# A 128x128 triangular inverse computed as two 64x64 diagonal blocks and one block below them

## The chip, the cores and the metric

One core of a Trainium2 chip runs the whole kernel. The metric is device time in microseconds (us), the median of three runs. Five engines work beside each other, each on its own queue of instructions and held by semaphores only: TensorE (PE, its weight loads shown apart as PEld), VectorE (DVE), ScalarE (ACT), GpSimd (POOL) and SyncE (SP), which issues the DMAs.

## What is computed

The reference is three layers over 256 tokens of width 1024: latent attention with a feed-forward part, differential attention with a feed-forward part, and a hybrid layer. The change is in the hybrid layer's delta rule, which works on 8 heads in chunks of 128 tokens, two chunks to a head:

```
m = jnp.where(strict, jnp.einsum('bhnid,bhnjd->bhnij', k_beta, kc) * decay, 0.0)
a_mat = m + jnp.eye(c, dtype=m.dtype)
rhs = jnp.concatenate([vc * bc[..., None], k_beta * jnp.exp(G)[..., None]], axis=-1)
sol = lax.linalg.triangular_solve(a_mat, rhs, left_side=True, lower=True, unit_diagonal=True)
u, w = sol[..., :dv], sol[..., dv:]
```

`a_mat` is 128x128, lower triangular with ones on the diagonal. All is float32.

## The kernel before

Everything is written out by hand per engine: each engine has a list of steps, the order in the code is its queue, and the steps wait on counters. Big projections split both operands into a high and a low float32r part (ScalarE writes `high`, line 342, VectorE or GpSimd writes `low`, line 349) and run three matmuls for each 128 rows of contraction (line 1508 in the delta-rule stage).

The delta rule goes over four pairs of heads, so four matrices at a time (two heads, two chunks). The inverse is made in the kernel by doubling: with the inverse of the diagonal blocks of size s known, the block below each is filled in. `inv` holds four inverses and, in its other half, their transposes. `masked_dve` makes the masked matrices `mk`, TensorE turns them (`turn_m_pe`), ScalarE copies them to `mt`. The blocks of size 2 need no matmul: a mask (`level1`) and a subtraction from the identity, for the inverses by GpSimd (`init_pool`, lines 1732 and 1735), for the transposes by VectorE (`init_dve`, lines 1697 and 1698). Then come six levels. A level is: x group (`level_x`, line 1745, four products of `mt` and `inv`), a masked copy by VectorE (`level_xm`, line 1758), t group (`level_t`, lines 1752 and 1753, eight products, four in the last level), and a subtraction by VectorE (`level_tt`, line 1763). Each product is 128x128x128 in plain float32.

While VectorE works between two groups, TensorE does half a projection of the next pair (`gdn_block`, 12 instructions), or of the following attention stage in the last pair. So `pair_pe` weaves groups and half projections, and `pair_dve` weaves the level steps with the convolution of the next pair. Behind the levels stand the state's matmuls (`f1` to `f4`), the output's norm and gate (`ogn`, line 1976; `og`, line 1984), and then, for the next pair, mask, turn and start values. TensorE fills the wait for these with matmuls that nobody reads (`spin`, line 482). Pairs run through `over`, a loop of the queue: the first pair and the last one or two are written out, the rest is the loop's body.

On GpSimd the end of a pair is: a power (line 2034), the low part of a weight chunk (slot 3), `init_pool`, `grow_pool` (`qdec_t`, line 1724), the low part of the next chunk (slot 4), the output's low part (`obl`, line 2047).

Of the kernel before, what the change touches and what calls it, by code (L numbers as in the profile page):

```python
# [23 lines left out]
P = 128  # L24
TOK = 256
# [17 lines left out]
LEVELS = 6  # L43

# [67 lines left out]
for _n, _w in (("ident", P), ("upper", P), ("strict_lower", P), ("level1", P), ("level1_t", P),  # L112
               ("levels", LEVELS * P), ("ones", P), ("causal", 3 * P), ("dist", NT * TOK),
               ("mla_cos", NT * MLA_ROPE), ("mla_sin", NT * MLA_ROPE), ("mla_rot", TOK),
               ("att_cos", NT * 2 * ROT), ("att_sin", NT * 2 * ROT)):
    _const(_n, _w)
# [3 lines left out]
def constants():  # L120
# [12 lines left out]
    def level(s):  # L133
        return (r // (2 * s) == k // (2 * s)) & (r % (2 * s) >= s) & (k % (2 * s) < s)

    put("level1", level(1))
    put("level1_t", level(1).T)
    put("levels", np.stack([level(2 << n) for n in range(LEVELS)], 1))
# [112 lines left out]
def build(nc, dram, y_out):  # L251
# [66 lines left out]
    def repeat(ap, n):  # L318

        return ap.unsqueeze(1).to_broadcast([P, n, ap.shape[1]])  # L320
# [1167 lines left out]
    level_of = cst("levels", "p (l k) -> p l k", l=LEVELS)  # L1488
# [76 lines left out]
    def is0(j):  # L1565
        return isinstance(j, int) and j == 0
# [126 lines left out]

    def init_dve(dve, j):
# [31 lines left out]
    def init_pool(pool, j):  # L1726

        pool.wait_ge(e_["mk"], j + 1)
        if not is0(j):
            pool.wait_ge(e_["f3"], j)  # L1730
        for e in range(2):
            last = pool.tensor_tensor(bm[:, 0, 2 * e:2 * e + 2, :], mk[:, e, 0, :, :], repeat(cst("level1"), NT), ALU.mult)
        last.then_inc(e_["bm"], 1)
        pool.wait_ge(e_["bm"], j + 1)
        pool.tensor_tensor(inv[:, 0, :, :], repeat(ident, 4), bm[:, 0, :, :], ALU.subtract).then_inc(e_["init_g"], 1)
# [12 lines left out]
    def level_t(pe, l, j):  # L1748
        pe.wait_ge(e_["xm"], LEVELS * j + l + 1)
        for c in range(4):  # L1750
            if l < LEVELS - 1:
                pe.matmul(A[2][:, c * P:(c + 1) * P], inv[:, 1, c, :], xm[:, c, :], start=True, stop=True)  # L1752
            last = pe.matmul(A[3][:, c * P:(c + 1) * P], xm[:, c, :], inv[:, 1, c, :], start=True, stop=True)  # L1753
        last.then_inc(e_["t"], 1)

    def level_xm(dve, l, j):
        dve.wait_ge(e_["x"], LEVELS * j + l + 1)
        dve.tensor_tensor(xm[:], quad(A[0]), repeat(level_of[:, l, :], 4), ALU.mult).then_inc(e_["xm"], 1)

    def level_tt(dve, l, j):  # L1760
        dve.wait_ge(e_["t"], LEVELS * j + l + 1)
        if l < LEVELS - 1:
            dve.tensor_tensor(inv[:].rearrange("p a c k -> p (a c k)"), inv[:].rearrange("p a c k -> p (a c k)"),
                              acc[:, 2:4, :].rearrange("p a b -> p (a b)"), ALU.subtract).then_inc(e_["tt"], 1)
        else:
            dve.tensor_tensor(inv[:, 1, :, :], inv[:, 1, :, :], quad(A[3]), ALU.subtract).then_inc(e_["tt"], 1)

    def pair_pe(pe, i):
# [13 lines left out]
        for e in range(2):  # L1782
            pe.matmul(A[0][:, e * P:(e + 1) * P], inv[:, 1, 2 * e, :], vbeta[:, 2 * e, :], start=True, stop=True)
        for e in range(2):
            last = pe.matmul(A[0][:, (2 + e) * P:(3 + e) * P], kbg[:, e, :], inv[:, 1, 2 * e + 1, :], start=True, stop=True)
# [14 lines left out]
        for e in range(2):  # L1800
            pe.matmul(A[0][:, e * P:(e + 1) * P], inv[:, 1, 2 * e + 1, :], vbeta[:, 2 * e + 1, :], start=True, stop=False)
            last = pe.matmul(A[0][:, e * P:(e + 1) * P], nwt[:, e, :], state[:, e, :], start=False, stop=True)
# [34 lines left out]
    def gdn_pe(pe):  # L1837
# [17 lines left out]
        over(pe, PAIRS, lambda i: pair_pe(pe, i))  # L1855
# [78 lines left out]
    def pair_dve(dve, i):  # L1934
# [42 lines left out]
        if more:  # L1977
            masked_dve(dve, i + 1)
        dve.wait_ge(e_["ot"], i + 1)
# [12 lines left out]
    def gdn_dve(dve):  # L1992
# [22 lines left out]
        masked_dve(dve, 0)  # L2015
        init_dve(dve, 0)
        over(dve, PAIRS, lambda i: pair_dve(dve, i), 2)

    def pair_pool(pool, i):
# [15 lines left out]
        if more:  # L2035
            refill(split, *source(3, 0, i + 1))
            init_pool(pool, i + 1)
# [11 lines left out]
    def gdn_pool(pool):  # L2049
# [9 lines left out]
        init_pool(pool, 0)  # L2059
# [624 lines left out]
```

## Time and profile before

| | us |
|---|---|
| median of three runs (1153.77 to 1156.37) | 1155.96 |
| the profiled execution | 1154.09 |
| its span | 1152.0 |
| TensorE busy | 1080.5 |
| VectorE busy | 696.5 |
| GpSimd busy | 428.6 |
| levels and starts of the four pairs | 729.7 to 929 of the span |

The profiled execution is one run; its span is from the first to the last recorded instruction. A row of a timeline gives the start in the span, the length, engine, line, operation, out<-in, the shape, and in brackets how long the engine stood idle before it and who released it. TensorE's instructions are pipelined, so that they overlap in their stamped lengths.

### The profile page before, as it was taken

What the parts mean: (1) busy time and instruction counts of PE and PEld (TensorE: products, weight loads), DVE (VectorE), ACT (ScalarE), POOL (GpSimd) and SP (SyncE); (2) the same over time, 40 slices, a digit from 0 to 9 for tenths busy, and PEclk for the clock granted to TensorE, in tenths of its full rate; (3) what the DMA queues carried; (4) which work ended last, traced back from release to release, by engine and by line L of the source; (5) the groups of instructions that cost most, each with busy time, mean ns of one, the idle gap of its engine ahead of it and who ended that gap; (6) DMA issues with size and microseconds to landing.
All of it is one profiled execution on the core that took longest, in us unless ns stands there. A gap on an engine that the chain in (4) does not pass through costs nothing.

```text
span 1152.0 us, 20992 instructions
## 1 busy us (share of the span) xinstructions
PE 1080.5 (94%) x7752; PEld 996.5 (86%) x7752; DVE 696.5 (60%) x1058; ACT 563.4 (49%) x1028; POOL 428.6 (37%) x296
## 2 busy tenths in 40 slices
PE   5699999999999998999999997989899999999997
PEld 5599699999978997699999966888888999999996
DVE  4455767667666556666766567566666555554444
ACT  4345565555555655555555555333333235544442
POOL 1000224333342332243343545647363345544331
PEclk9899999999999999999999999999999999999999
DMA  8233366565534442556555333131312234445551
GB/s 336 72 114 112 140 204 193 182 205 185 180 110 144 140 136 74 183 185 198 187 189 172 128 110 128 38 111 37 110 41 69 80 106 164 146 146 188 187 188 40
DMA packets 46256, 162.94 MB, mean 141 GB/s; under 512 B 5248, under 2 KB 5504, under 8 KB 46080
## 3 DMA queue, kind: packets, MB, share of 16 engines
q1 hardware_dynamic: 44768, 157.05, 40.8%
q0 software_dynamic: 1440, 5.24, 1.4%
q8 instruction: 31, 0.51, 0.2%
q14 instruction: 17, 0.14, 0.0%
HBM read 161.22 MB, written 1.05 MB: 141 GB/s over the span
## 4 chain that ended last, share of the span: by engine, by line
PE 83%; DVE 9%; ACT 3%; POOL 2%; issue 2%; DMA 1%; DVEq 0%; POOLq 0%; ACTq 0%
PE work L377 13%; PE work L379 13%; PE work L378 13%; PE acc L377 5%; PE acc L378 5%; PE acc L379 5%; PE work L1508 5%; PE work L2095 4%; PE work L2107 2%; PE acc L1745 2%; PE acc L1753 2%; DVE silu L1553 2%; PE acc L2107 1%; DVE conv L1543 1%; PE acc L1752 1%
## 5 line engine op out<-in xcount | busy, mean ns | idle before, releaser
L349 POOL TENSOR_TENSOR low<-raw,high 128x1024 fp32r<-128x1024 f32 x109 | 265.7, 2439 | 336.2 <-ACT high L342 336.2
L349 DVE TENSOR_TENSOR low<-raw,high 128x1024 fp32r<-128x1024 f32 (+2 forms) x191 | 277.8, 1463 | 166.3 <-ACT high L342 166.2
L342 ACT ACTIVATE high<-raw 128x1024 fp32r<-128x1024 f32 (+4 forms) x301 | 306.1, 1025 | 45.9 <-DMA raw<-in_w_out 21.9
L377 PE MATMUL work<-xh,high 128*128 128x256 f32 (+1 forms) x1032 | 292.2, 283 | 0.3 <-DVE low L349 0.3
L378 PE MATMUL work<-xl,high 128*128 128x256 f32 (+1 forms) x1032 | 288.7, 280 | 0.0
L379 PE MATMUL work<-xh,low 128*128 128x256 f32 (+1 forms) x1032 | 288.5, 280 | 0.0
L377 PEld LDWEIGHTS work<-xh,high 128*128 128x128 f32 (+1 forms) x1032 | 194.0, 188 | 5.3 <-issue 2.9
L378 PEld LDWEIGHTS work<-xl,high 128*128 128x128 f32 (+1 forms) x1032 | 194.1, 188 | 2.5 <-issue 0.7
L379 PEld LDWEIGHTS work<-xh,low 128*128 128x128 f32 (+1 forms) x1032 | 194.0, 188 | 0.2
L1044 POOL TENSOR_TENSOR h<-gelu,cv 128x256 f32<-128x256 f32 x44 | 48.8, 1108 | 200.5 <-ACT gelu L964 106.7
L1508 PE MATMUL work<-xh,high 128*128 128x256 f32 x256 | 76.9, 301 | 3.6 <-DVE hn L1563 2.0
L1508 PE MATMUL work<-xl,high 128*128 128x256 f32 x256 | 72.0, 281 | 0.0
L1508 PE MATMUL work<-xh,low 128*128 128x256 f32 x256 | 71.8, 281 | 0.0
L377 PE MATMUL acc<-high,hh 128*128 128x512 f32 x168 | 65.9, 392 | 1.2 <-DVE low L349 1.2
L378 PE MATMUL acc<-low,hh 128*128 128x512 f32 x168 | 65.8, 392 | 0.0
L379 PE MATMUL acc<-high,hl 128*128 128x512 f32 x168 | 65.4, 389 | 0.0
L970 ACT ACTIVATE hh<-h 128x256 fp32r<-128x256 f32 x44 | 18.4, 418 | 70.1 <-POOL h L1044 70.1
L1508 PEld LDWEIGHTS work<-xh,high 128*128 128x128 f32 x256 | 49.0, 192 | 4.2 <-issue 2.2
L958 ACT ACTIVATE cv<-work,vec 128x256 f32<-128x256 f32 x44 | 24.8, 564 | 51.0 <-PE work L379 51.0
L1508 PEld LDWEIGHTS work<-xl,high 128*128 128x128 f32 x256 | 48.9, 191 | 0.0
L1508 PEld LDWEIGHTS work<-xh,low 128*128 128x128 f32 x256 | 48.7, 190 | 0.0
L1046 POOL TENSOR_TENSOR hl<-h,hh 128x256 fp32r<-128x256 f32 x44 | 34.0, 773 | 24.4 <-ACT hh L970 24.4
(364 smaller groups left out, 2345.7 us busy)
## 6 DMA issues: line engine op xcount, KB each, us to landing
raw<-in_w_ffn SPq DMA_DIRECT2D x132, 512.0 KB, 4.2
raw<-in_w_out SPq DMA_DIRECT2D x39, 512.0 KB, 4.1
raw<-in_w_diff SPq DMA_DIRECT2D x32, 512.0 KB, 3.9
raw<-in_w_att SPq DMA_DIRECT2D x32, 512.0 KB, 3.8
raw<-in_w_gdn SPq DMA_DIRECT2D x24, 512.0 KB, 3.4
raw<-in_w_mla SPq DMA_DIRECT2D x8, 512.0 KB, 3.3
raw<-in_w_gdnz SPq DMA_DIRECT2D x8, 512.0 KB, 4.5
raw<-in_w_mla SPq DMA_DIRECT2D x8, 384.0 KB, 3.1
```

The lines of the kernel that those rows point to most:

```text
L342: act.activation(high[k][:, 0:w], raw[k][:, 0:w], ACT.Copy).then_inc(high_done[k], 1)
L349: eng.tensor_tensor(low[k][:, 0:w], raw[k][:, 0:w], high[k][:, 0:w], ALU.subtract).then_inc(low_done[k], 1)
L377: pe.matmul(out, lhs[0], rhs[0], start=start, stop=False)
L378: pe.matmul(out, lhs[0], rhs[1], start=False, stop=False)
L379: return pe.matmul(out, lhs[1], rhs[0], start=False, stop=stop)
L958: act.activation((cg, cv)[value][j][:], W[bank][:, 0:TOK], ACT.Identity, scale=ffn_taps(layer, i, j, value, 1, 0), bias=ffn_taps(layer, i, ...
L1044: pool.tensor_tensor(h32[j][:], gelu[j][:], cv[j][:], ALU.mult).then_inc(s["h32"], 1)
L1046: pool.tensor_tensor(hl[j][:], h32[j][:], hh[j][:], ALU.subtract).then_inc(s["hl"], 1)
L1508: last = pe.matmul(W[x][:, 0:TOK], l[slot][:, b * P:(b + 1) * P], r[:, b, :], start=(s == 0), stop=(s == 23))
L1553: dve.scalar_tensor_tensor(silu2[:, 3 * e + x, :], tanh_[x][:], 1.0, conv[x][:], ALU.add, ALU.mult).then_inc(taps[x]["silu"], 1)
L2095: last = pe.matmul(W[0][:, t * TOK:(t + 1) * TOK], x[:, b, t * P:(t + 1) * P], w[k][:, o:o + TOK], start=(b == 0 and term == 0), stop=(b = ...
L2107: last = pe.matmul(out, w[k][:, b * P:(b + 1) * P], x[:, b, :], start=(s == 0), stop=(s == 23))
```

## The change

The 128x128 inverse is now two inverses of 64x64, on partitions 0 to 63 and 64 to 127, and one block below. The levels up to 64 treat the two diagonal blocks as separate 64x64x64 products: the lower half of the partitions uses rows and columns 0 to 63 of TensorE's array, the upper half 64 to 127. `inv`, `xm` and the masks have 64 columns in place of 128, so VectorE's masked copy and subtraction cover half the elements; both results of a t group lie in one PSUM bank. The last level fills the one lower block: four products in its x group, four in its t group, an unmasked copy, and a multiply by -1 into `inv_t`, a new 128x128 tile of the transposed inverses. Its diagonal blocks are copied from `inv` at the end of the fifth level, and its zero block is set once.

The rows' start values move from GpSimd (`init_pool`, gone) to VectorE (`init_rows_dve`, directly behind `masked_dve`). Steps that mask a diagonal block are now two instructions of 64 partitions. TensorE's pairs are written out four times in place of the loop.

```diff
-                  "levels", LEVELS * P                     (each level's mask 128 wide)
+                  "levels", (LEVELS - 1) * HALF            (64 wide; ident_half, level1, level1_t too)
-    inv = sb("inv", [P, 2, 4, P])
+    inv = sb("inv", [P, 2, 4, HALF])
+    inv_t = sb("inv_t", [P, 4, P])
-    xm = sb("xm", [P, 4, P])
+    xm = sb("xm", [P, 4, HALF])
+    def init_rows_dve(dve, j):
+        dve.wait_ge(e_["mk"], j + 1)
+        for h_ in HALVES:
+            last = dve.tensor_tensor(bm[h_, 0, :, 0:HALF]..., mk[h_, :, 0, :, h_], cst("level1")[h_, :]..., ALU.mult)
+        last.then_inc(e_["bm"], 1)
+        dve.wait_ge(e_["bm"], j + 1)
+        dve.tensor_tensor(inv[:, 0, :, :], repeat(cst("ident_half"), 4), bm[:, 0, :, 0:HALF],
+                          ALU.subtract).then_inc(e_["init_g"], 1)
     def init_dve(dve, j):
         dve.wait_ge(e_["mtev"], j + 1)
-        chain(dve.tensor_tensor(bm[:, 1, :, :], mt[:], repeat(cst("level1_t"), 4), ALU.mult))
-        chain(dve.tensor_tensor(inv[:, 1, :, :], repeat(ident, 4), bm[:, 1, :, :], ALU.subtract))
+        if is0(j):
+            dve.memset(inv_t[HALF:P, :, 0:HALF], 0.0)
+        for h_ in HALVES:
+            last = dve.tensor_tensor(bm[h_, 1, :, 0:HALF], mt[h_, :, h_], repeat(cst("level1_t")[h_, :], 4), ALU.mult)
+        chain(last)
+        chain(dve.tensor_tensor(inv[:, 1, :, :], repeat(cst("ident_half"), 4), bm[:, 1, :, 0:HALF], ALU.subtract))
-    def init_pool(pool, j):
...
     def level_x(pe, l, j):
+        lower, upper = HALVES
         for c in range(4):
-            last = pe.matmul(A[0][:, c * P:(c + 1) * P], mt[:, c, :], inv[:, 0, c, :], start=True, stop=True)
+            at = slice(c * HALF, (c + 1) * HALF)
+            if l < LEVELS - 1:
+                for h_ in HALVES:
+                    last = pe.matmul(A[0][h_, at], mt[h_, c, h_], inv[h_, 0, c, :], start=True, stop=True)
+            else:
+                last = pe.matmul(A[0][upper, at], mt[lower, c, upper], inv[lower, 0, c, :], start=True, stop=True)
     def level_t(pe, l, j):
         for c in range(4):
+            at, at_t = slice(c * HALF, (c + 1) * HALF), slice((4 + c) * HALF, (5 + c) * HALF)
             if l < LEVELS - 1:
-                pe.matmul(A[2][:, c * P:(c + 1) * P], inv[:, 1, c, :], xm[:, c, :], start=True, stop=True)
-            last = pe.matmul(A[3][:, c * P:(c + 1) * P], xm[:, c, :], inv[:, 1, c, :], start=True, stop=True)
+                for h_ in HALVES:
+                    pe.matmul(A[2][h_, at], inv[h_, 1, c, :], xm[h_, c, :], start=True, stop=True)
+                for h_ in HALVES:
+                    last = pe.matmul(A[2][h_, at_t], xm[h_, c, :], inv[h_, 1, c, :], start=True, stop=True)
+            else:
+                last = pe.matmul(A[2][lower, at], xm[upper, c, :], inv[upper, 1, c, :], start=True, stop=True)
     def level_tt(dve, l, j):
+            if l == LEVELS - 2:
+                dve.wait_ge(e_["tt"], LEVELS * j + l + 1)
+                for h_ in HALVES:
+                    dve.tensor_copy(inv_t[h_, :, h_], inv[h_, 1, :, :])
         else:
-            dve.tensor_tensor(inv[:, 1, :, :], inv[:, 1, :, :], quad(A[3]), ALU.subtract).then_inc(e_["tt"], 1)
+            dve.tensor_scalar(inv_t[0:HALF, :, HALF:P], quad_half(A[2][0:HALF, 0:4 * HALF]), -1.0, None,
+                              ALU.mult).then_inc(e_["tt"], 1)
-        over(pe, PAIRS, lambda i: pair_pe(pe, i))
+        for i in range(PAIRS):
+            pair_pe(pe, i)
         if more:
             masked_dve(dve, i + 1)
+            init_rows_dve(dve, i + 1)
         if more:
             refill(split, *source(3, 0, i + 1))
-            init_pool(pool, i + 1)
             grow_pool(pool, i + 1)
```

TensorE, the t group of a level and the last instruction of the half projection ahead of it. Before:

```order
L1508 MATMUL work<-xh,low 128x256
L1752 MATMUL acc<-xm,inv 128x128
L1753 MATMUL acc<-inv,xm 128x128
L1752 MATMUL acc<-xm,inv 128x128
L1753 MATMUL acc<-inv,xm 128x128
```

And now:

```order
L1516 MATMUL work<-xh,low 128x256
L1771 MATMUL acc<-xm,inv 64x64 x2
L1773 MATMUL acc<-inv,xm 64x64 x2
L1771 MATMUL acc<-xm,inv 64x64 x2
L1773 MATMUL acc<-inv,xm 64x64 x2
```

Each 128x128 product has become two of 64x64, first the one on the lower half, then the one on the upper; the half projections around them stay where they were. (A row is a product; each is two instructions on the engine.)

VectorE, from the output's norm to the start values of the next pair. Before:

```order
L1976 TENSOR_TENSOR ogn<-acc,root 128x512
L1690 TENSOR_TENSOR mk<-acc,mask_e 128x512 x2
L1984 SCALAR_TENSOR_TENSOR og<-acc,gdn_gain,hn 128x512
L1563 SCALAR_TENSOR_TENSOR hn<-tanh,work 128x256
L1697 TENSOR_TENSOR bm<-mt,const 128x512
L1698 TENSOR_TENSOR inv<-const,bm 128x512
```

And now:

```order
L1698 TENSOR_TENSOR mk<-acc,mask_e 128x512 x2
L1705 TENSOR_TENSOR bm<-mk,const 64x4x64 x2
L1709 TENSOR_TENSOR inv<-const,bm 128x256
L2017 SCALAR_TENSOR_TENSOR og<-acc,gdn_gain,hn 128x512
L1571 SCALAR_TENSOR_TENSOR hn<-tanh,work 128x256
L1718 TENSOR_TENSOR bm<-mt,const 64x4x64 x2
L1720 TENSOR_TENSOR inv<-const,bm 128x256
```

Three instructions have come in ahead of the gated output `og`, and the columns' start values are three instructions in place of two.

GpSimd at the same place. Before:

```order
L2034 TENSOR_TENSOR root<-mean,vec 128x4
L349 TENSOR_TENSOR low<-raw,high 128x1024
L1732 TENSOR_TENSOR bm<-mk,const 128x256 x2
L1735 TENSOR_TENSOR inv<-const,bm 128x512
L1724 TENSOR_TENSOR qdec_t<-silu,grown_all 128x256
L349 TENSOR_TENSOR low<-raw,high 128x1024
L2047 TENSOR_TENSOR obl<-og,obh 128x512
```

And now:

```order
L2068 TENSOR_TENSOR root<-mean,vec 128x4
L352 TENSOR_TENSOR low<-raw,high 128x1024
L1746 TENSOR_TENSOR qdec_t<-silu,grown_all 128x256
L352 TENSOR_TENSOR low<-raw,high 128x1024
L2080 TENSOR_TENSOR obl<-og,obh 128x512
```

The two steps of the start values are gone, so the second low part and the steps behind it have moved up.

## Rows read from the trace of the kernel before

**Rows 1.** The page: engine totals, and the last chain's shares by engine.

```profile
PE 1080.5 (94%) x7752; PEld 996.5 (86%) x7752; DVE 696.5 (60%) x1058; ACT 563.4 (49%) x1028; POOL 428.6 (37%) x296
...
PE 83%; DVE 9%; ACT 3%; POOL 2%; issue 2%; DMA 1%; DVEq 0%; POOLq 0%; ACTq 0%
```

**Rows 2.** Grouped lines, TensorE, the inversion: xcount | busy us, mean ns | idle before.

```profile
L1753 PE MATMUL acc<-inv,xm 128*128 128x128 f32 x192 | 35.1, 275 | 0.0
L1752 PE MATMUL acc<-xm,inv 128*128 128x128 f32 x160 | 30.9, 275 | 0.0
...
L1745 PE MATMUL acc<-inv,mt 128*128 128x128 f32 x192 | 27.5, 286 | 2.1 <-DVE inv L1763 1.3 <-DVE inv L1698 0.8
```

**Rows 3.** Timeline, TensorE, one level of pair 0: start us, length us, instruction.

```profile
735.29 1.16 PE L1745 MATMUL acc<-inv,mt 128*128 128x128 f32 x8
...
737.71 0.38 PE L1752 MATMUL acc<-xm,inv 128*128 128x128 f32 x2
...
739.27 0.39 PE L1753 MATMUL acc<-inv,xm 128*128 128x128 f32 x2
...
740.97 1.16 PE L1745 MATMUL acc<-inv,mt 128*128 128x128 f32 x8
```

**Rows 4.** Timeline, TensorE: two 16-row transposes between projection instructions.

```profile
683.41 0.28 PE L1508 MATMUL work<-xl,high 128*128 128x256 f32 x1
683.53 0.27 PE L1508 MATMUL work<-xh,low 128*128 128x256 f32 x1
683.74 0.29 PE L1381 MATMUL work<-const,junk 16*128 16x16 f32 x2
683.96 0.39 PE L1508 MATMUL work<-xh,high 128*128 128x256 f32 x1
684.18 0.28 PE L1508 MATMUL work<-xl,high 128*128 128x256 f32 x1
```

**Rows 5.** Waits of TensorE, 726 to 937 us: us in total, times, longest.

```profile
PE acc L1745 <- DVE inv L1763: 1.3, 3, 0.4
PE acc L1745 <- DVE inv L1698: 0.8, 2, 0.5
```

**Rows 6.** Timeline, VectorE, between pairs 0 and 1.

```profile
778.35 1.28 DVE L1690 TENSOR_TENSOR mk<-acc,mask_e 128x512 f32<-128x512 f32 x2
780.15 0.75 DVE L1984 SCALAR_TENSOR_TENSOR og<-acc,gdn_gain,hn 128x512 f32<-128x512 f32 x1 [0.53 <-PE acc L1827]
780.82 0.41 DVE L1563 SCALAR_TENSOR_TENSOR hn<-tanh,work 128x256 f32<-128x256 f32 x1
781.56 1.77 DVE L1697 TENSOR_TENSOR bm<-mt,const 128x512 f32<-128x512 f32 x1 [0.33 <-ACT mt L1635]
783.37 1.09 DVE L1698 TENSOR_TENSOR inv<-const,bm 128x512 f32<-128x512 f32 x1
```

**Rows 7.** Timeline, TensorE, the filler between these pairs and the x group behind it.

```profile
780.39 3.60 PE L482 MATMUL acc<-const 128*128 128x512 f32 x8
784.52 0.38 PE L1745 MATMUL acc<-inv,mt 128*128 128x128 f32 x1 [0.53 <-DVE inv L1698]
```

**Rows 8.** Timeline, TensorE's weight loads, two products with 16 moving columns.

```profile
695.66 0.31 PEld L1386 LDWEIGHTS work<-gate_g,const 128*128 128x128 f32 x2
695.88 0.30 PEld L1387 LDWEIGHTS work<-gate_g,const 128*128 128x128 f32 x2
```

**Rows 9.** Timeline, ScalarE, two places: before the transposes, between the pairs.

```profile
681.04 0.37 ACT L1397 ACTIVATE junk<-work 16x256 f32<-16x256 f32 x1 [3.99 <-PE work L379]
...
779.99 1.05 ACT L342 ACTIVATE high<-raw 128x1024 fp32r<-128x1024 f32 x1
```

**Rows 10.** Timeline, GpSimd, between pairs 0 and 1.

```profile
777.67 2.38 POOL L349 TENSOR_TENSOR low<-raw,high 128x1024 fp32r<-128x1024 f32 x1
780.02 1.41 POOL L1732 TENSOR_TENSOR bm<-mk,const 128x256 f32<-128x256 f32 x2
781.51 1.27 POOL L1735 TENSOR_TENSOR inv<-const,bm 128x512 f32<-128x512 f32 x1
782.75 1.17 POOL L1724 TENSOR_TENSOR qdec_t<-silu,grown_all 128x256 f32<-128x256 f32 x1
783.88 2.81 POOL L349 TENSOR_TENSOR low<-raw,high 128x1024 fp32r<-128x1024 f32 x1
```

**Rows 11.** Busy us of a stretch: length, engines, granted clock, DMA share, GB/s.

```profile
828.00:831.40 3.40, 3.40 (x20) 3.40 (x18) 1.01 (x3) 1.23 (x3) 0.00 (x0) 0.55 0.16 61
```

More of the change, by code:

```diff
@@ L43 @@
 LEVELS = 6
+HALF = 64
 class Phase:
@@ L109, in _const @@
     CONST[name] = (sum(w for _, w in CONST.values()), width)
-for _n, _w in (("ident", P), ("upper", P), ("strict_lower", P), ("level1", P), ("level1_t", P),
-               ("levels", LEVELS * P), ("ones", P), ("causal", 3 * P), ("dist", NT * TOK),
+for _n, _w in (("ident", P), ("upper", P), ("strict_lower", P), ("ident_half", HALF), ("level1", HALF),
+               ("level1_t", HALF), ("levels", (LEVELS - 1) * HALF), ("ones", P), ("causal", 3 * P), ("dist", NT * TOK),
                ("mla_cos", NT * MLA_ROPE), ("mla_sin", NT * MLA_ROPE), ("mla_rot", TOK),
@@ L133, in level @@
     def level(s):
-        return (r // (2 * s) == k // (2 * s)) & (r % (2 * s) >= s) & (k % (2 * s) < s)
+        full = (r // (2 * s) == k // (2 * s)) & (r % (2 * s) >= s) & (k % (2 * s) < s)
+        return full[:, 0:HALF] | full[:, HALF:P]
+    put("ident_half", (r == k)[:, 0:HALF] | (r == k)[:, HALF:P])
     put("level1", level(1))
-    put("level1_t", level(1).T)
-    put("levels", np.stack([level(2 << n) for n in range(LEVELS)], 1))
+    put("level1_t", np.concatenate([level(1)[0:HALF].T] * 2))
+    put("levels", np.stack([level(2 << n) for n in range(LEVELS - 1)], 1))
     put("ones", np.ones((P, P)))
@@ L318, in repeat @@
     def repeat(ap, n):
-        return ap.unsqueeze(1).to_broadcast([P, n, ap.shape[1]])
+        return ap.unsqueeze(1).to_broadcast([ap.shape[0], n, ap.shape[1]])
     landed = [sem(f"landed{k}") for k in range(6)]
@@ L1487, in build, with quad_half @@
     A = [acc[:, k, :] for k in range(4)]
-    level_of = cst("levels", "p (l k) -> p l k", l=LEVELS)
+    level_of = cst("levels", "p (l k) -> p l k", l=LEVELS - 1)
+    HALVES = (slice(0, HALF), slice(HALF, P))
+    def quad_half(a):
+        return a.rearrange("p (c k) -> p c k", c=4)
     BLOCKS = [(0, 0), (1, 0), (2, 0), (0, 1), (1, 1), (2, 1)]
@@ L1724, in grow_pool @@
         pool.tensor_tensor(qdec_t[:], qk_t[:, :, 1, :], g2, ALU.mult).then_inc(e_["grown"], 1)
-    def init_pool(pool, j):
[L1728 to L1735, printed above, removed]
     def level_x(pe, l, j):
@@ L1749, in level_t @@
         pe.wait_ge(e_["xm"], LEVELS * j + l + 1)
+        lower, upper = HALVES
         for c in range(4):
+            at, at_t = slice(c * HALF, (c + 1) * HALF), slice((4 + c) * HALF, (5 + c) * HALF)
             if l < LEVELS - 1:
[L1752 to L1753 removed]
+                for h_ in HALVES:
[4 more added lines that the diff above has]
+                last = pe.matmul(A[2][lower, at], xm[upper, c, :], inv[upper, 1, c, :], start=True, stop=True)
         last.then_inc(e_["t"], 1)
@@ L1757, in level_xm @@
         dve.wait_ge(e_["x"], LEVELS * j + l + 1)
-        dve.tensor_tensor(xm[:], quad(A[0]), repeat(level_of[:, l, :], 4), ALU.mult).then_inc(e_["xm"], 1)
+        if l < LEVELS - 1:
+            dve.tensor_tensor(xm[:], quad_half(A[0][:, 0:4 * HALF]), repeat(level_of[:, l, :], 4),
+                              ALU.mult).then_inc(e_["xm"], 1)
+        else:
+            dve.tensor_copy(xm[HALF:P, :, :], quad_half(A[0][HALF:P, 0:4 * HALF])).then_inc(e_["xm"], 1)
     def level_tt(dve, l, j):
@@ L1782, in pair_pe @@
         for e in range(2):
-            pe.matmul(A[0][:, e * P:(e + 1) * P], inv[:, 1, 2 * e, :], vbeta[:, 2 * e, :], start=True, stop=True)
+            pe.matmul(A[0][:, e * P:(e + 1) * P], inv_t[:, 2 * e, :], vbeta[:, 2 * e, :], start=True, stop=True)
         for e in range(2):
-            last = pe.matmul(A[0][:, (2 + e) * P:(3 + e) * P], kbg[:, e, :], inv[:, 1, 2 * e + 1, :], start=True, stop=True)
+            last = pe.matmul(A[0][:, (2 + e) * P:(3 + e) * P], kbg[:, e, :], inv_t[:, 2 * e + 1, :], start=True, stop=True)
         last.then_inc(e_["f1"], 1)
@@ L1800, in pair_pe @@
         for e in range(2):
-            pe.matmul(A[0][:, e * P:(e + 1) * P], inv[:, 1, 2 * e + 1, :], vbeta[:, 2 * e + 1, :], start=True, stop=False)
+            pe.matmul(A[0][:, e * P:(e + 1) * P], inv_t[:, 2 * e + 1, :], vbeta[:, 2 * e + 1, :], start=True, stop=False)
             last = pe.matmul(A[0][:, e * P:(e + 1) * P], nwt[:, e, :], state[:, e, :], start=False, stop=True)
@@ L2015, in gdn_dve @@
         masked_dve(dve, 0)
+        init_rows_dve(dve, 0)
         init_dve(dve, 0)
```

5 lines of the change are left out of this document (3 added, 2 removed).

## The prediction, made before the changed kernel ran

> **What bounds the kernel now.** I read the page from the top: TensorE is busy 94% of the span and carries 83% of the chain that ended last, VectorE 9% [rows 1]. So most of what leaves TensorE shortens the run, and what VectorE loses counts only where TensorE waits for it. The grouped lines give the part that the change touches: the three matmul lines of the inversion are 192 + 160 + 192 = 544 TensorE instructions, two for each float32 product [rows 2]. Then the timeline of one level, from one x group to the next (735.29 to 740.97, 5.68 us) [rows 3]: x group, half a projection (12 instructions), t group, half a projection. From 737.71 to 739.27 lie 14 instructions of the t group: 1.56 / 14 = 0.1114 us each. The stamped length of an instruction is more than twice that, since they are pipelined; pace is what counts. A projection instruction has a pace of 0.117 us (683.41 to 683.53 and its neighbours) [rows 4]. A level thus holds 24 x 0.1114 + 24 x 0.117 = 5.48 us of work and 0.20 us of gaps. The reader is to see that VectorE is almost never the limit inside a level: in the whole stage TensorE waited 1.3 us in three places for the subtraction that ends a level [rows 5]. Between two pairs it is different: VectorE's chain runs there (mask, gated output, start values), and the first x group starts 0.53 us late behind it [rows 6, 7].
>
> **The change, part by part.** Durations are of the profiled execution, 1154.09 us (span 1152.0); the three timed runs have a median of 1155.96, 1.87 above it.
>
> *Matmuls of the levels.* 544 instructions of 128 by 128 become (5 x 24 + 8) x 2 x 4 = 1024 of 64 by 64: four pairs, 24 products in each of five levels, 8 in the last. What has to be known is the pace of a small one, and no row shows it. The nearest rows: a product with only 16 moving columns, but 128 columns of weights, still goes at 0.11 us (two weight loads from 695.66, the next two from 695.88) [rows 8]. So a full float32 instruction is held by its weight load as much as by its 128 moving columns, and both halve at 64. Lower bound: the loads and matmuls of opposite corners run side by side, a quarter of the pace, 0.028. Upper bound: an instruction costs 0.111 whatever its size. I take half the pace, 0.0555, loads passing one behind another, because [rows 8] are the only ones where something small was tried and there the load set the pace. 1024 x 0.0555 = 56.8 against 544 x 0.1114 = 60.6: -3.8 us (bounds -31.9 and +53.1).
>
> *Changing the shape of the array.* Each x and t group is now an island of corner products between full-size projections, 2 x 6 x 4 = 48 islands. One island stands in the trace: two transposes of 16 rows between projection instructions [rows 4]. Their ScalarE input was ready 2.3 us before (681.04 + 0.37) [rows 9], so it is not a wait. From the last projection before (683.53) to the second behind (684.18) pass 0.65 us; 0.117 + 2 x 0.11 + 0.117 = 0.46 would do. So 0.19 us for in and out: 48 x 0.19 = 9.1 us. The 0.20 of gaps in 20 levels (4.0) and the waits of 1.3 go into that, the waits because the subtraction has half the elements (1024 to 512). Net +3.8 us. Matmuls and islands together: 0.0 us.
> The Trainium skill, "TensorEngine Tiling (Array Packing)", section Tiling Modes, Key Properties, speaks against the change: a switch of the tiling mode drains TensorE. The 0.19 is less than two whole drains: an instruction is stamped 0.28 and paced 0.12, so a full one would be 0.16 at each end and 96 of them 15.4 us in place of 9.1. By the page the time would be some 6 us above mine; the row decides.
>
> *Start values move from GpSimd to VectorE.* Before, GpSimd masks the rows' start values (two parts of bm, then inv) while VectorE goes on to the gated output and the columns' start values [rows 6, 10]. Now VectorE does both, in the order mask, rows' values (three instructions), gated output, gate product, columns' values (three). Each of the six has half the elements of one of 128x512, whose pace is 0.6 (two in 1.28) [rows 6]: half of that and a little for the start, 0.34 each, an estimate. All six read two SBUF operands, and the rows show what that means beside GpSimd: VectorE's bm at 781.56 took 1.77 us, until GpSimd's inv (781.51 + 1.27) was done, GpSimd's next then took 1.17 for 256 elements, and its 1024-column subtraction at 783.88 took 2.81, the end of VectorE's inv (784.46) plus 2.25 [rows 6, 10]. They take turns, instruction by instruction. Worked through for pair 0 to 1: the mask ends at 779.63; GpSimd's subtraction holds on to 780.05; first row part to 780.39, GpSimd's qdec_t to 780.98, second row part to 781.32; then GpSimd's next subtraction, no longer behind its own start values and ready with ScalarE's high part (779.99 + 1.05 = 781.04) [rows 9], holds to 783.57; rows' inv to 783.9; gated output 784.6; gate product 785.0; columns' values 786.1, or 787.3 if GpSimd's last step of the pair (obl) falls between. The x group started at 784.52, so it starts 1.6 to 2.8 us later; I take +2.0 for this and the next pair, and +1.0 for the third, where no second subtraction of that slot stands on GpSimd (the weights of slot 4 end there). +5.0 us. If nothing collides, the x group stands right behind the filler (780.39 + 8 x 0.43 = 783.83; the 0.43 from 3.60 less the last one's tail, over 8) [rows 7]: bound -0.8, the waits for inv that the stage has now [rows 5]. Upper bound: 2 x 2.8 + 1.3 = 6.9, and if TensorE's clock falls behind the longer wait, as its grant stood at a mean of 0.55, nearly all at 1.2 GHz, for 3.4 us between pairs 1 and 2 [rows 11], 1.7 us each: 12. Queued behind the six on VectorE is the whole pair: TensorE's x group, then everything. Before pair 0 the same work is hidden by the filler, with no GpSimd work left beside it.
>
> *At nothing.* VectorE's xm and subtraction at half size: covered already by a 1.4 us half projection; without that cover they would be worth 0.9 a level. The two copies to inv_t in level 4 lie under the following half projection. GpSimd's three instructions less: it only makes its next subtraction earlier, counted above. TensorE's pairs written out four times: the loop's branch lay behind the filler; cost 0, bounds 1 us either way. The constants' DMA is smaller, at the start, beside other loads.
>
> Sum: -3.8 + 3.8 + 5.0 = +5.0 us: 1159.1 on the profiled run, 1161.0 on the median.
>
> **The rivals.**
> *A, the corners work side by side (faster).* The products alternate between the two corners, which share neither rows nor columns nor output partitions. If both weight loads and matmuls of the two overlap, the pace falls to 0.028 and the levels to 1024 x 0.028 = 28.7: -31.9 + 3.8 + 5.0 = -23, 1133. With some issue cost left, 0.034: 34.8, -17, 1139; 0.04: 1145. It decides from a pace below 0.0506 on, where the levels have paid for the starts of the pairs. For it: rows of the array are only read by their own corner, and a level of 4.5 us would still leave VectorE and ScalarE time. Against: [rows 8], one load behind the other; and the two instructions of a product lie next to each other on the same corner.
> The Trainium skill, "TensorEngine Tiling (Array Packing)", Key Properties, has this rule: different tiles can load weights and multiply in parallel. No run here shows it; by it the time would be this rival's.
> *B, a small instruction has a price of its own.* If the pace does not fall below 0.07 to 0.08: +11 to +21 for the matmuls, 1175 to 1186 in all, taken as 1181. For it: load and matmul of 64 columns are two issues each in 0.0555 us, and no two in the trace are that close. Against: nothing in the rows looks like an issue limit.
> *C, VectorE is not held.* GpSimd's subtraction comes later or elsewhere; the starts of the pairs gain 0.8, the levels are even: 1155.2, no change.
>
> **How the numbers follow.** Forecast 0.42, its own range 1152 to 1173 (paces 0.052 to 0.060: -3.6 to +4.6; pair starts from -0.8 to 12). A 0.36, B 0.14, C 0.08. Predicted 1161.0. Range 1132 to 1174: it leaves out the best end of A (0.04), nearly all of B (0.12) and 0.02 of the forecast. Some 0.2% (2.3 us) is what a measurement can tell from no change. Faster: 0.35 of A, 0.03 of C, 0.01 of the forecast: 0.39. Same: 0.01 of A, 0.05 of C, 0.05 of the forecast: 0.11. Slower: 0.36 and B: 0.50.
>
> **What would show it.** The t group of a level (32 instructions): 1.78 us if the pace is 0.0555, about 0.9 in A, over 2.2 in B. The distance from x group to x group: 5.68 now, about 5.7 here, 4.5 in A. The island's edges: weight loads of the first projection instruction behind a t group start after it, not during it. Between pairs: VectorE's rows' values with spans well over 0.4 us, the first x group 4 us or more behind the filler's last instruction. Wrong I am if the t group's starts come in twos, or if VectorE's six instructions show their bare 0.4.

## The result

| kernel | us, median | range | runs | ratio to before, 95% interval |
|---|---|---|---|---|
| before | 1155.31 | 1153.77 to 1156.37 | 4 | |
| changed | 1147.03 | 1145.71 to 1148.30 | 4 | 0.9929 [0.9912, 0.9947] |

The change is faster by 8.3 us, where 1161.0 was forecast: the range held the time, the direction was wrong. A second, longer comparison gave the same (1147.11, 0.9931 [0.9912, 0.9950], label e10_after_again below).

The profiled execution of the changed kernel took 1148.30 us, its span 1146.5. Its page answers to [rows 1]; TensorE has more instructions (8232) and less busy time:

```profile
PE 1069.9 (93%) x8232; PEld 978.2 (85%) x8232; DVE 694.3 (61%) x1083; ACT 563.5 (49%) x1028; POOL 415.5 (36%) x284
```

A row of a timeline stands for instructions that the profile has put together: in x4 below, four, two products. TensorE in pair 0, which answers to [rows 3]: from the last projection instruction ahead of the first level's t group to the x group of the third level.

```profile
734.46 0.28 PE L1516 MATMUL work<-xh,low 128*128 128x256 f32 x1
734.67 0.33 PE L1771 MATMUL acc<-xm,inv 64*64 64x64 f32 x4
734.84 0.28 PE L1773 MATMUL acc<-inv,xm 64*64 64x64 f32 x4
...
735.54 0.28 PE L1773 MATMUL acc<-inv,xm 64*64 64x64 f32 x4
735.75 0.39 PE L1516 MATMUL work<-xh,high 128*128 128x256 f32 x1
735.97 0.28 PE L1516 MATMUL work<-xl,high 128*128 128x256 f32 x1
...
737.37 0.68 PE L1759 MATMUL acc<-inv,mt 64*64 64x64 f32 x16
737.98 0.39 PE L1516 MATMUL work<-xh,high 128*128 128x256 f32 x1
...
742.29 0.68 PE L1759 MATMUL acc<-inv,mt 64*64 64x64 f32 x16
```

Four instructions start every 0.117 us (734.84 to 735.54 is 24 instructions in 0.70): **0.029 us each**, about a quarter of the 0.1114 before, not half. The single records behind these rows start in twos, one on each corner: 734.779 and 734.786, then 734.838 and 734.844. A level is 742.29 - 737.37 = 4.92 us long, 5.68 before. The islands cost more than forecast: from 734.46 to 735.97 pass 1.51 us, of which two projection steps (0.234) and 32 x 0.029 = 0.93 are work, so that 0.35 is the way in and out.

The last level has its products on one corner only. In the x group of that level 8 instructions take as long as 16 on two corners (757.05 to 757.65, against 737.37 to 737.98):

```profile
756.84 0.28 PE L1516 MATMUL work<-xh,low 128*128 128x256 f32 x1
757.05 0.67 PE L1761 MATMUL acc<-inv,mt 64*64 64x64 f32 x8
757.65 0.39 PE L1516 MATMUL work<-xh,high 128*128 128x256 f32 x1
```

Between the pairs it went the other way. TensorE's waits in the stage (728 to 937 us; us in total, times, longest), against the 0.8 and 1.3 of [rows 5]:

```profile
PE acc L1759 <- DVE inv L1720: 7.1, 3, 3.1
PE work L1591 <- DVE silu L1561: 5.7, 3, 1.9
```

The second was there before too. The first is new: VectorE's start values are late, by 3.07, 3.07 and 0.99 us. VectorE between pairs 0 and 1, which answers to [rows 6]:

```profile
777.93 1.55 DVE L1705 TENSOR_TENSOR bm<-mk,const 64x256 f32<-64x256 f32 x2
779.52 2.50 DVE L1709 TENSOR_TENSOR inv<-const,bm 128x256 f32<-128x256 f32 x1
...
783.80 1.37 DVE L1720 TENSOR_TENSOR inv<-const,bm 128x256 f32<-128x256 f32 x1
```

and GpSimd beside it, which answers to [rows 10]:

```profile
779.38 2.35 POOL L352 TENSOR_TENSOR low<-raw,high 128x1024 fp32r<-128x1024 f32 x1 [0.18 <-ACT high L345]
783.42 1.47 POOL L2080 TENSOR_TENSOR obl<-og,obh 128x512 fp32r<-128x512 f32 x1 [1.69 <-ACT obh L1935]
```

L1709 and L1720, of 128x256, take 2.50 and 1.37 us, and each ends 0.3 us after the GpSimd instruction beside it (781.73, 784.89).

The stage by its pairs, from the first x group of one pair to that of the next, and in the last pair to the x group of the last level: 54.78, 56.16, 55.44 and 29.44 before, 52.87, 54.29, 53.18 and 25.92 now, 9.6 us less in all. The medians differ by 8.3. The rest lies outside the stage. What comes ahead of it differs between the profiles by up to 5 us in both directions: the stage of this profile began 2.7 us later than that of before, that of another changed version (e8 below) 0.2 earlier. What comes behind it took 1.3 us more than before in this profile.

### The profile page after: what moved, and what is told of

Its sections match the earlier page's. It is cut to its first block, busy times and chain, and to the rows that moved or that the text cites. A ratio compares the mean times of both kernels' runs of the same rounds, so it can differ in the third digit from the quotient of the medians.

```text
span 1146.5 us, 21927 instructions
## 1 busy us (share of the span) xinstructions
PE 1069.9 (93%) x8232; PEld 978.2 (85%) x8232; DVE 694.3 (61%) x1083; ACT 563.5 (49%) x1028; POOL 415.5 (36%) x284
## 4 chain that ended last, share of the span: by engine, by line
PE 81%; DVE 8%; issue 4%; POOL 3%; ACT 3%; DMA 1%; DVEq 0%; POOLq 0%; ACTq 0%
PE work L380 13%; PE work L381 13%; PE work L382 13%; PE work L1516 6%; PE acc L380 5%; PE acc L381 5%; PE acc L382 5%; PE work L2127 4%; PE work L2139 3%; PE acc L2139 1%; POOL low L352 1%; PE acc L1771 1%; PE acc L1759 1%; PE work L1137 1%; PE acc L1773 1%
```

## The experiments

Nine runs follow; e10 is the changed kernel once more. "Before" in each row of this table is the median of the kernel before on the same chip.

| label | us, median | range | before | ratio, 95% interval |
|---|---|---|---|---|
| e1_corners_apart | 1169.1 | 1166.99 to 1170.1 | 1155.07 | 1.0117 [1.0095, 1.0139] |
| e2_before_rows_vector | 1165.95 | 1165.34 to 1168.63 | 1155.07 | 1.0101 [1.0078, 1.0124] |
| e3_rows_gpsimd | 1140.51 | 1140.06 to 1141.23 | 1155.07 | 0.9875 [0.9855, 0.9894] |
| e4_gpsimd_later | 1144.19 | 1143.6 to 1145.16 | 1155.07 | 0.9908 [0.9891, 0.9925] |
| e5_corner_island | 1162.44 | 1162.28 to 1164.93 | 1154.81 | 1.0064 [1.0047, 1.0081] |
| e6_full_island | 1157.05 | 1153.03 to 1157.84 | 1154.81 | 1.0014 [1.0003, 1.0026] |
| e8_silu_free | 1129.5 | 1129.15 to 1131.73 | 1154.81 | 0.9785 [0.9767, 0.9804] |
| e9_before_silu_free | 1146.32 | 1143.57 to 1147.47 | 1155.54 | 0.9915 [0.9885, 0.9944] |
| e10_after_again | 1147.11 | 1145.91 to 1151.19 | 1155.54 | 0.9931 [0.9912, 0.9950] |

The theory after the result: the two corners load and multiply side by side, which is worth more than the islands and the late starts cost together; all three are real and separate.

### Do the corners work side by side, or is a small product just quick? (e1)

The changed kernel, with all products of the lower corner first and then all of the upper one, in the five levels that have both. The work is the same, only neighbours in the queue are on one corner.

```diff
+        for h_ in HALVES if l < LEVELS - 1 else ():
             for c in range(4):
                 at = slice(c * HALF, (c + 1) * HALF)
-                for h_ in HALVES:
-                    last = pe.matmul(A[0][h_, at], mt[h_, c, h_], inv[h_, 0, c, :], ...)
+                last = pe.matmul(A[0][h_, at], mt[h_, c, h_], inv[h_, 0, c, :], ...)
     (level_t likewise)
```

> The changed kernel, but in the first five levels all products of the lower corner are issued first, then all of the upper one. Theory (the two corners work side by side when neighbours in the queue lie on opposite corners; one corner alone has a pace of 0.058 us an instruction, as the last level's x group suggests, 8 instructions on one corner in the time of 16 on two): the pace goes from 0.029 to 0.058, 48 x 0.029 = 1.4 us a level, 20 levels: +28 us on 1147, about 1175; a t group's instructions take 1.8 us in place of 0.93. Rival (a 64x64 instruction costs 0.029 by its size alone, wherever it lies): no change, 1147.

It took 1169.1 us, 22 more than the changed kernel: 20 levels at 1.00 us more each, and in its stage five stretches of some 3.4 us at a granted clock of 0.50 (1.2 GHz) in place of three. A level of pair 0:

```profile
736.83 0.96 PE L1758 MATMUL acc<-inv,mt 64*64 64x64 f32 x16
737.72 0.38 PE L1516 MATMUL work<-xh,high 128*128 128x256 f32 x1
...
739.49 0.28 PE L1771 MATMUL acc<-inv,xm 64*64 64x64 f32 x2
739.61 0.28 PE L1770 MATMUL acc<-xm,inv 64*64 64x64 f32 x2
...
742.75 0.96 PE L1758 MATMUL acc<-inv,mt 64*64 64x64 f32 x16
```

Now two instructions start in each 0.117 us, 0.058 each, and the level is 742.75 - 736.83 = 5.92 us long, longer than before the change. So the gain below half of a full instruction comes not from the small product but from its neighbour on the other corner. (Whether two corners that share rows or columns would do the same, no run shows.) The run came out 6 us below the theory's 1175, and the trace shows where: in the middle of the t group, where the queue passes from the lower corner to the upper one, eight instructions take 0.29 us in place of 0.47:

```profile
740.07 0.33 PE L1770 MATMUL acc<-xm,inv 64*64 64x64 f32 x4
740.19 0.33 PE L1771 MATMUL acc<-inv,xm 64*64 64x64 f32 x4
740.36 0.28 PE L1770 MATMUL acc<-xm,inv 64*64 64x64 f32 x2
```

The two corners overlap there for once. 0.18 us in each of 40 groups are 7.2 us.

### What does the move of the rows' start values cost by itself? (e2)

The kernel before, with `init_pool` called on VectorE behind `masked_dve`, at its full width, ahead of pair 0 too; nothing else is changed.

```diff
     (pair_dve)     masked_dve(dve, i + 1)
+                   init_pool(dve, i + 1)
     (pair_pool)    refill(split, *source(3, 0, i + 1))
-                   init_pool(pool, i + 1)
```

> The kernel before, with one part of the change alone: the rows' start values move from GpSimd to VectorE, at full width (three more VectorE instructions between mask and gated output). Theory (VectorE is held there by GpSimd's second subtraction, which has moved up): the first x group of pairs 1 to 3 starts 3 to 4 us behind the filler twice and about 2 once, 8 us in all, and a half-clock stretch may follow: 1163 to 1167 on 1155.3. Rival (only VectorE's own added work counts, 2 x 0.34 + 0.6 = 1.3 a pair): +4, 1159.

1165.95 us, 10.9 over before. TensorE's wait for the start values in the stage, and the longest row of VectorE between pairs 0 and 1:

```profile
PE acc L1745 <- DVE inv L1698: 8.0, 3, 3.3
```
```profile
780.98 2.76 DVE L1735 TENSOR_TENSOR inv<-const,bm 128x512 f32<-128x512 f32 x1
```

Waits of 8.0 against 0.8 are 7.2 us; behind two of the late starts the granted clock then lies at 0.50, 1.2 GHz, for 3.4 us (from 787.1 and from 848.6), and its stage holds four such stretches where before has two. This part of the change loses time on its own.

### The same taken back in the changed kernel (e3), and GpSimd's subtraction alone moved (e4)

e3 gives the rows' start values back to GpSimd, at the new half size and at their old place in its list; its `init_rows_pool` also waits for GpSimd's own step ahead of each of its steps. e4 leaves them on VectorE and only puts GpSimd's second subtraction (slot 4) behind `obl`.

```diff
 e3, pair_dve:
-            init_rows_dve(dve, i + 1)
 e3, pair_pool:
+            init_rows_pool(pool, i + 1)
             grow_pool(pool, i + 1)
 e4, pair_pool:
             grow_pool(pool, i + 1)
-            refill(split, *source(3, 1, i + 1))
         ...
         pool.tensor_tensor(obl[:, pair, :], og32[:], obh[:, pair, :], ALU.subtract).then_inc(e_["ol"], 1)
+        if more:
+            refill(split, *source(3, 1, i + 1))
```

> The changed kernel, but the rows' start values are on GpSimd again, ahead of qdec_t as before, at half size. Theory (held by GpSimd's subtraction): the waits of 7.1 us before the first x groups fall to about 1, and the half-clock stretches behind them go, 1.5 each: about 1139 against 1147. Rival (VectorE's own work, 3 x 0.34 = 1.0 a pair): -3, 1144.

> The changed kernel with VectorE's work untouched; on GpSimd the second subtraction of a pair's end (the low part of slot 4) stands behind the output's low part, so it can't fall between VectorE's start values. Theory (it is that subtraction that holds VectorE): the waits of 3.07 us at the starts of pairs 1 and 2 fall to about 0.5, the third (0.99, no such subtraction) stays, half-clock stretches go: 1140 to 1142. Rival (VectorE's own work): 1147.

e3 took 1140.51, 6.5 less than the changed kernel, and the 7.1 us of waits for the start values are gone: the x group (784.74) stands right behind the filler (781.21, 3.60 long). The low clock, which was expected to go too, did not: e3 has three such stretches in the stage as the changed kernel has, all behind the waits for `silu`. e4 took 1144.19, 2.8 less. VectorE in e4, and TensorE's wait:

```profile
781.62 0.43 DVE L1709 TENSOR_TENSOR inv<-const,bm 128x256 f32<-128x256 f32 x1
...
783.83 1.37 DVE L1720 TENSOR_TENSOR inv<-const,bm 128x256 f32<-128x256 f32 x1
```
```profile
PE acc L1759 <- DVE inv L1720: 2.9, 3, 1.0
```

L1709 has fallen from 2.50 to 0.43 without a change of its own: GpSimd's subtraction held it. No semaphore stands between the two, so "held by semaphores only", said of the engines at the start, is not the whole of it. The rest of the wait, 0.9 to 1.0 at each of the three starts, is VectorE's own three instructions, of which the two of L1705 still take 1.50 us beside `qdec_t`, and `obl`, which still lies beside L1720; how it divides among them, no run shows. e4 missed its 1140 to 1142 by 2 us. Waits of 2.9 us were left where 2.0 had been counted, and the low clock did not go: e4 too has three stretches in the stage, all behind the waits for `silu`.

### What does an island cost? (e5, e6)

The changed kernel, with one more product that nobody reads in the middle of each of the 36 half projections of pairs 0 to 2: in e5 of 64x64 on the lower corner, in e6 with weights of 128x128 and 64 moving columns.

```diff
     (gdn_block, behind the sixth group of three)
+  e5:  pe.matmul(A[3][0:HALF, 0:HALF], cst("ident")[0:HALF, 0:HALF], cst("ident")[0:HALF, 0:HALF], ...)
+  e6:  pe.matmul(A[3][:, 0:HALF], ident, cst("ident")[:, 0:HALF], ...)
```

> The changed kernel with one more 64x64 product, read by nobody, in the middle of each of the 36 half projections that are woven into the levels of pairs 0 to 2: 36 new islands, with no wait in them. Theory (the 0.345 us that an island costs in the trace of the changed kernel is the change of the array's shape itself): 36 x (0.345 + 2 x 0.058) = 16.6 us, 1163.6. Rival (the edge costs the 0.19 us of the prediction, and the rest of the 0.345 was a wait for VectorE's masked copy or subtraction): 36 x (0.19 + 0.116) = 11 us, 1158. In the timeline: two projection instructions around the product 0.58 us apart against 0.42.

> The same place and count, but the product has weights of the full 128x128 and 64 moving columns, so that the array keeps its shape. Theory (only the change of shape costs): 36 x 2 x 0.117 = 8.4 us at most, 1155.4, less if 64 columns are quicker than 128. Rival (any foreign float32 product between the projections costs an edge, whatever its shape): the same as with the small product, 1158 to 1164.

e5 and e6 took 15.4 and 10.0 us more than the changed kernel, 0.43 and 0.28 for each product. The timeline tells them apart more sharply. e5, the step before the product to the second behind:

```profile
738.77 0.28 PE L1518 MATMUL work<-xh,low 128*128 128x256 f32 x1
738.98 0.32 PE L1517 MATMUL acc<-const 64*64 64x64 f32 x2
739.24 0.38 PE L1518 MATMUL work<-xh,high 128*128 128x256 f32 x1
739.46 0.28 PE L1518 MATMUL work<-xl,high 128*128 128x256 f32 x1
```

and e6:

```profile
738.04 0.28 PE L1518 MATMUL work<-xh,low 128*128 128x256 f32 x1
738.15 0.33 PE L1517 MATMUL acc<-const 128*128 128x64 f32 x2
738.29 0.37 PE L1518 MATMUL work<-xh,high 128*128 128x256 f32 x1
738.50 0.28 PE L1518 MATMUL work<-xl,high 128*128 128x256 f32 x1
```

0.69 us in e5, 0.46 in e6, of which 0.234 are the two projection steps. The small product thus costs 0.456, its own 2 x 0.058 and 0.34 for the edges; the full one costs 0.226, its own 2 x 0.113 and nothing besides. Whole levels of pair 0, with two of these products each, agree: 5.79 us in e5 and 5.35 in e6 against 4.92, 0.435 and 0.215 a product. The distance that the first expectation names, between the two projection instructions around the product, is 0.47 (738.77 to 739.24), between its 0.58 and its 0.42: part of the price falls on the next step, to 739.46, 0.22 us where 0.117 is usual. Both steps together decide, 0.69 against 0.695 by the theory and 0.54 by the rival.

It is the change of the array's shape that costs, not a foreign product, and no wait is in it. By weight loads one sees how: in the changed kernel the load of the next instruction normally runs ahead of its matmul, and at an island's edge it does not. Weight loads of the changed kernel around the t group of 734.67:

```profile
734.35 0.19 PEld L1516 LDWEIGHTS work<-xh,low 128*128 128x128 f32 x1
734.67 0.19 PEld L1771 LDWEIGHTS acc<-xm,inv 64*64 64x64 f32 x4
...
735.48 0.20 PEld L1773 LDWEIGHTS acc<-inv,xm 64*64 64x64 f32 x4
735.75 0.19 PEld L1516 LDWEIGHTS work<-xh,high 128*128 128x128 f32 x1
```

Ahead of an instruction within a group its load is 0.11 us earlier (734.35 for the matmul of 734.46); the first load of the island (734.67) and the first behind it (735.75) start with their matmuls. The measured total of e6, 1157.05, lies above the "1155.4 at most" of its theory, and 1.9 above the 8.1 us that its rows give. In its profile TensorE also waits three times, 1.7 us in all, for VectorE's subtraction, which the changed kernel doesn't show (one level of pair 0 takes 5.97 us in place of 5.35); the stage is 9.4 us longer. So the remainder is about this wait, though its runs spread by 4.8 us. The 15.4 of e5 is less sharp than its rows as well: its stage has five stretches of low clock in place of three, and one fewer lies behind it.

### A version that goes on (e8), and its part without the change (e9)

The three waits for `silu` (5.7 us, in both kernels) look like the one that e4 took away: VectorE's `silu` takes 2.43 us beside GpSimd's subtraction for the last convolution block. e8 is e3 with that subtraction behind VectorE's `qk_tok`; e9 is the kernel before with this edit alone.

```diff
             root_pool(pool, i + 1)
+            pool.wait_ge(e_["tk"], i + 2)
             refill(split, *source(*BLOCKS[5], i + 1))
```

> The version with the rows' start values back on GpSimd at half size (1140.5), and GpSimd's subtraction for the last convolution block's weight slot put behind VectorE's qk_tok, so that it no longer lies beside VectorE's silu (2.43 us there, 0.41 elsewhere). Theory (VectorE is held by GpSimd's subtraction, and TensorE's three waits of 1.9 us for silu come from that): the three waits go, -5.7 us, and with them some of the half-clock stretches behind them (1.7 us each): 1130 to 1135. Rival (the silu would be late anyway, by ScalarE's tanh and VectorE's convolution ahead of it): 1139 to 1141.

> The kernel before with that one edit alone: GpSimd's subtraction for the last convolution block's weight slot behind VectorE's qk_tok. It was worth 11 us (1140.5 to 1129.5) behind the changed levels. Theory (it has nothing to do with the levels, the same three waits for silu stand in the trace of before, 1.9 us each): about -11 us here too, 1142 to 1146. Rival (with levels 0.75 us longer VectorE stands less in the way, so part of it was a follow-up of the change): -6 us or less, 1149 or more.

e8 took 1129.5 us, 11.0 less than e3 and 2.15% less than before: the fastest of all. e3 (VectorE, GpSimd):

```profile
767.94 2.43 DVE L1561 SCALAR_TENSOR_TENSOR silu<-tanh,conv 128x256 f32<-128x256 f32 x1 [0.48 <-ACT tanh L1542]
...
767.74 2.35 POOL L352 TENSOR_TENSOR low<-raw,high 128x1024 fp32r<-128x1024 f32 x1
```

and e8:

```profile
764.10 0.42 DVE L1561 SCALAR_TENSOR_TENSOR silu<-tanh,conv 128x256 f32<-128x256 f32 x1 [0.48 <-ACT tanh L1542]
...
766.17 2.47 DVE L1689 TENSOR_TENSOR kdec<-qk_tok,gate_kd 128x256 f32<-128x256 f32 x1
...
766.00 2.35 POOL L352 TENSOR_TENSOR low<-raw,high 128x1024 fp32r<-128x1024 f32 x1 [2.08 <-DVE qk_tok L1678]
```

The hold has not gone, it has moved to `kdec` (2.47 us), for which nobody waits. Each of the three pairs became 3.2 to 3.3 us shorter (51.34, 51.22, 51.20 to 48.05, 47.97, 47.94). Of that 1.9 is the wait. Most of the rest is TensorE's clock, which in e3 fell behind this wait in all three pairs and in e8 in none. Windows, whose last three figures are granted clock, DMA share and GB/s: of e3, behind the first of these waits (0.58 behind the other two also), then of e8, its three pairs whole:

```profile
772.00:775.40 3.40, 3.40 (x21) 3.40 (x20) 1.37 (x4) 1.09 (x2) 0.00 (x0) 0.58 0.22 90
```
```profile
722.00:780.00 58.00, 57.20 (x598) 48.62 (x600) 38.45 (x67) 20.02 (x36) 34.94 (x26) 1.00 0.23 74
780.00:825.00 45.00, 44.26 (x504) 39.71 (x500) 33.43 (x59) 19.42 (x35) 27.34 (x19) 1.00 0.28 95
825.00:880.00 55.00, 54.00 (x628) 47.85 (x627) 37.79 (x65) 18.59 (x34) 29.47 (x21) 1.00 0.24 80
```

In e3 TensorE stood still twice, 1.92 and 0.75 us with 0.66 of work between, and the grant then lay at 0.58 in this window, most of it at 1.2 GHz. From the start of the products that wait for `qk_tok` (L1599) to the fourth projection instruction behind them pass 4.25 us (771.83 to 776.08); in e8 only the wait of 0.74 is left, the grant stays at 1.00 throughout, and the same work takes 2.62 (765.98 to 768.60): 1.6 us. 1.9 + 1.6 is 0.2 to 0.3 more than the pairs gained; that is lost again between the output's matmuls (L1862) and the next x group (4.41 us in e3, 4.74 in e8). The Trainium skill, "SBUF — State Buffer", section Terms, says that VectorE and GpSimd share one port pair, held for a whole instruction, and that the loser stands still; the 2.43 against 0.42 here, and 2.50 against 0.43 in e4, agree.

e9 took 9.2 us less than before, 0.3 us past the slow end of the theory: most of the 11 us have nothing to do with the levels. The 1.8 us between are about the price of one low stretch: before has two of them in the stage, e3 three, e8 and e9 none. Beside it, e8 says what the changed levels are worth without the late starts: 1146.3 - 1129.5 = 16.8 us, and the two stages differ by as much (186.9 and 170.1).

### Once more (e10)

> The changed kernel once more, on the same chip as the run beside it. Theory: 1147, as at first. Rival (what the first comparison showed hangs on the chip that it ran on): outside 1144 to 1150. Its profile gives a second reading of the level period (4.92 us at first) and of the three waits for the start values (7.1 us).

1147.11 us; the level of pair 0 again 4.92 (736.54 to 741.46), the waits for the start values 6.8 us. The first comparison holds.

The loop of TensorE's pairs in place of the written-out pairs was not tried; what that part costs stays open. In the stage, the sum below leaves 0.2 us for it and for all else that it doesn't name.

## Why the prediction was wrong, by its steps

| step | predicted | measured |
|---|---|---|
| matmuls of the levels | -3.8 | 960 x 0.029 + 64 x 0.058 = 31.6, against 60.6: **-29.0** |
| islands, less gaps and waits | +3.8 | 48 x 0.345 = 16.6, less 4.0 and 1.3: **+11.3** |
| start values on VectorE | +5.0 | waits 7.1 in place of 0.8: **+6.3** |
| clock | only in the bound | one low stretch more: **+1.6** |
| sum | +5.0 | -9.8; the stage lost 9.6 |

That the range held 1147 is luck as far as the steps go. The gain of the matmuls was put 25.2 us too low, and the cost of islands, starts and clock 7.5, 1.3 and 1.6 us too low; the second error took back part of the first. No branch of the prediction has these terms together.

**The step that failed is the matmul pace**, "I take half the pace, 0.0555, loads passing one behind another". The number itself was good for one corner: it measured 0.058, in the last level and all through e1. The wrong part was to let [rows 8] decide between the forecast and rival A. Those are loads of the full array, 128 rows by 128 columns, and no two of them lie on separate corners. They could speak on the size of a product and not on its neighbour, and the prediction named them as evidence against A all the same. The second argument against A, that the two instructions of a product lie next to each other on the same corner, did not hold either: the pattern lower, lower, upper, upper already gives 0.029. This one reading is worth 25 us and turned the sign. The Trainium skill, "TensorEngine Tiling (Array Packing)", section Tiling Modes, Key Properties, says that different tiles can load weights and multiply in parallel; the 0.029 on two corners against 0.058 on one agrees, where the prediction had left it to a rival. Its own sign of being wrong, starts that come in twos, is what the trace shows.

**The islands had the right mechanism and the wrong size**, 0.19 against 0.345. The Trainium skill, "TensorEngine Tiling (Array Packing)", section Tiling Modes, Key Properties, says that a switch of the tiling mode drains TensorE; e5 against e6 agrees, and the 15.4 us for whole drains, which the prediction set beside its 9.1 and passed over, is close to the 16.6 measured. The 0.19 came out of [rows 4] with two small transposes at 0.11 each. At the 0.058 of a small instruction on one corner the same rows give 0.65 - 0.234 - 0.116 = 0.30, close to what was measured: the term was held down by the price taken for a small instruction. Rival A, at the pace that came, sums to 1155.96 - 29.0 + 3.8 + 5.0 = 1135.8; with the measured sizes of the other terms, 7.5 (islands), 1.3 (starts) and 1.6 (clock) more, it is 1146.2, against 1147.0.

**The start values went as worked through.** Starts 2, 2 and 1 us later than before were forecast; waits of 3.07, 3.07 and 0.99 in place of 0.53, 0.24 and none make them 2.5, 2.8 and 1.0 later. GpSimd's subtraction did get in ahead of the rows' inv (L1709, 2.50), and `obl` did fall beside the columns' values (L1720, 1.37), the two collisions that the text names. e2, e3 and e4 show this step from three sides. Rival C, VectorE not held, fell with it; e3 is what it would have been, and better than its 1155 because of the levels.

**The clock** stood in the upper bound, and came: the grant lay at 0.53 and 0.56 behind the first two late starts, and at 0.52 from a wait for `silu` on in the third pair. Before there were two such stretches, 0.55 [rows 11] and 0.57, both behind that wait. One more is 3.4 x (1 - 0.53) = 1.6 us. That the late starts brought it is not shown: e3 and e4, with no late starts or shorter ones, have three stretches too, all behind the waits for `silu`, and e3 gained 6.5 us where the waits alone are 7.1. Windows of the changed kernel, the last two behind the waits for `silu` of the first two pairs:

```profile
785.90:789.30 3.40, 3.40 (x28) 3.15 (x26) 0.42 (x1) 0.00 (x0) 0.00 (x0) 0.53 0.00 0
840.30:843.60 3.30, 3.30 (x28) 3.08 (x30) 0.42 (x1) 0.00 (x0) 0.00 (x0) 0.56 0.00 0
878.10:881.50 3.40, 2.90 (x14) 2.50 (x14) 2.81 (x6) 0.13 (x1) 0.00 (x0) 0.52 0.02 5
...
770.00:773.40 3.40, 2.66 (x24) 2.50 (x23) 2.44 (x6) 1.11 (x3) 0.00 (x0) 1.00 0.52 154
824.00:827.40 3.40, 2.65 (x25) 2.42 (x24) 2.75 (x6) 1.06 (x2) 0.00 (x0) 1.00 0.52 154
```

The same wait, 1.9 and 0.75 us, is followed by full clock there and by half of it a pair later. Between each two pairs the clock of the changed kernel fell once, behind one of the two waits; what decides which, no run here tells.

**What was costed at nothing** stayed there as far as the trace shows it (TensorE's pairs written out have no run of their own): no wait for VectorE's masked copies or subtractions stands among TensorE's waits in the stage, although a level is 0.76 us shorter, and the copies to `inv_t` held nobody. Rival B has no support: on one corner a small instruction takes half the time of a full one.

The signs "the distance from x group to x group: 5.68 now, about 5.7 here, 4.5 in A" and "1.78 us if the pace is 0.0555, about 0.9 in A" were the right ones to look at: 4.92 and 0.93, between the two for the level because of the islands, and plainly A for the pace.

## What to carry to other kernels

Ask of every row that is used as a bound which resource it shows: a pace of two full-size loads says nothing on two loads that share no row or column of the array. Where small products alternate between opposite corners they come four to one full product, but each visit between full-size products costs a price of its own (0.345 us here), so it pays to make the visits few and long. And work moved to VectorE has to be placed by what GpSimd does beside it: the same instruction was 0.43 or 2.50 us long by that alone, and moving one GpSimd instruction was worth 11.0 us (e8 against e3; 9.2 on the kernel before), more than the 8.3 of the whole change.

## What the runs showed of the hardware that was not expected

- A float32 64x64 product with 64 columns on alternating corners: 0.029 us an instruction; on one corner 0.058; a full one 0.1114. The order in the queue alone decides between the first two (e1: 1.00 us a level, 22 us in all).
- Going from the full array to a corner and back costs 0.32 to 0.35 us (e5, the changed kernel), and the first weight load at each edge starts with its matmul, not ahead of it. A full-size product at the same place costs no edge (0.456 against 0.226 us).
- TensorE's clock does not fall behind each wait of the same length: 1.9 and 0.75 us were followed by a grant of 0.58 in e3 and by 1.00 in two pairs of the changed kernel, where a later wait of 3 us then brought 0.53. Without waits over 0.75 us in the first three pairs (e8, e9) it stood at 1.00 all through them.
